# Expert weights of an MoE layer: from split fp32r passes over a short ring to plain fp32 matmuls in column halves and quarters over one ring of 14 slots

## What is computed

```python
def moe_swiglu(h, router, w_in, w_out):
    logits = (hf @ router).astype(jnp.float32)            # 256 tokens, 8 experts
    top_v, top_i = lax.top_k(logits, TOP_K)               # TOP_K = 2
    gates = jnp.sum(jax.nn.one_hot(top_i, N_EXPERTS) * softmax(top_v)[..., None], axis=1)
    for e in range(N_EXPERTS):                            # w_in[e]: 1024 x 7168, w_out[e]: 3584 x 1024
        y = y + gates[:, e:e + 1] * swiglu(hf, w_in[e], w_out[e])
```

## Time and profile before

| | us |
|---|---|
| median of 3 runs (lowest, highest) | 1541.47 (1537.42, 1542.13) |
| the profiled execution | 1540.51 |
| its span, first to last instruction | 1538.8 |
| TensorE busy in it | 1463.6 |
| VectorE busy in it | 1148.2 |
| ScalarE busy in it | 810.3 |

### The profile page before, as it was taken

One profiled execution on the slowest core, in us unless ns is written; L12 is line 12 of the kernel. 1 busy time (PEld: TensorE's weight loads), 2 busy tenths in 40 slices (PEclk: granted clock), 3 DMA queues, 4 the chain that ended last, 5 costly groups with the idle time before them and its releaser, 6 DMA issues.

```text
span 1538.8 us, 20581 instructions
## 1 busy us (share of the span) xinstructions
PE 1463.6 (95%) x6931; PEld 1077.8 (70%) x6931; DVE 1148.2 (75%) x1406; ACT 810.3 (53%) x986; POOL 62.2 (4%) x47
## 2 busy tenths in 40 slices
PE   5999999999999999999999999899998999999997
PEld 5788877888878977756666667575665766666665
DVE  6989998887888878756676677584767756676687
ACT  2544545444446657645464555463645645564565
POOL 0222300000000120000000000000000000000000
PEclk9999999999999999999999999999999999999999
DMA  9987676888976352999999999899999999999993
GB/s 329 346 295 259 248 271 235 300 284 311 320 258 209 106 207 102 335 357 396 400 387 396 398 387 391 317 394 397 398 396 352 361 395 397 397 380 399 396 392 138
DMA packets 220826, 501.51 MB, mean 326 GB/s; under 512 B 9744, under 2 KB 40640, under 8 KB 206400
## 3 DMA queue, kind: packets, MB, share of 16 engines
q1 hardware_dynamic: 219568, 500.29, 88.0%
q10 hardware_dynamic: 1168, 0.07, 0.0%
HBM read 499.28 MB, written 1.05 MB: 325 GB/s over the span
## 4 chain that ended last, share of the span: by engine, by line
PE 55%; DMA 19%; DVE 15%; issue 6%; ACT 4%; DVEq 0%; SPq 0%; ACTq 0%
DMA raw<-in_moe_w_in 13%; PE ps L615 12%; PE ps L617 11%; PE ps L616 11%; PE ps L1155 6%; DVE acc L1916 4%; DMA ada<-in_ada_w 3%; PE ps L1191 3%; DVE w_lo L1897 3%; ACT w_hi L1762 2%; DMA raw<-in_moe_w_out 2%; DVE w_lo L2364 2%; PE ps L915 1%; PE ps L917 1%; PE ps L919 1%
## 5 line engine op out<-in xcount | busy, mean ns | idle before, releaser
L2364 DVE TENSOR_TENSOR w_lo<-raw,w_hi 128x1024 fp32r<-128x1024 f32 x411 | 482.8, 1219 | 156.5 <-ACT w_hi L1762 155.5
L1762 ACT ACTIVATE w_hi<-raw 128x1024 fp32r<-128x1024 f32 x411 | 417.6, 1053 | 195.9 <-DMA raw<-in_moe_w_out 90.1
L615 PE MATMUL ps<-w_hi,RA 128*128 128x512 f32 x1008 | 405.8, 403 | 22.7 <-DVE w_lo L2364 15.7
L617 PE MATMUL ps<-w_hi,RA 128*128 128x512 f32 x1008 | 394.6, 391 | 0.0
L616 PE MATMUL ps<-w_lo,RA 128*128 128x512 f32 x1008 | 394.2, 391 | 0.0
L615 PEld LDWEIGHTS ps<-w_hi,RA 128*128 128x128 f32 x1008 | 190.3, 189 | 88.0 <-DVE w_lo L2364 39.0
L1897 DVE TENSOR_TENSOR w_lo<-raw,w_hi 128x1024 fp32r<-128x1024 f32 x171 | 214.3, 1263 | 13.6 <-ACT w_hi L1435 13.1
L1435 ACT ACTIVATE w_hi<-raw 128x1024 fp32r<-128x1024 f32 x171 | 174.8, 1053 | 88.1 <-PE ps L617 55.4
L617 PEld LDWEIGHTS ps<-w_hi,RA 128*128 128x128 f32 x1008 | 189.9, 188 | 41.2
L616 PEld LDWEIGHTS ps<-w_lo,RA 128*128 128x128 f32 x1008 | 190.3, 189 | 37.2 <-issue 0.7
L1916 DVE SCALAR_TENSOR_TENSOR acc<-ada,cond,acc 128x512 f32<-128x512 f32 x189 | 152.1, 805 | 3.7 <-DMA ada<-in_ada_w 0.7
(11 more groups left out here) (337 smaller groups left out, 1351.7 us busy)
## 6 DMA issues: line engine op xcount, KB each, us to landing
raw<-in_moe_w_in SPq DMA_DIRECT2D x224, 1024.0 KB
raw<-in_moe_w_out SPq DMA_DIRECT2D x112, 1024.0 KB
ada<-in_ada_w SPq DMA_DIRECT2D x46, 1024.0 KB, 7.4
raw<-in_ff_w_in SPq DMA_DIRECT2D x44, 512.0 KB
raw<-in_ret_w_in SPq DMA_DIRECT2D x16, 1024.0 KB
raw<-in_ff_w_out SPq DMA_DIRECT2D x11, 1024.0 KB
raw<-in_ret_w_in SPq DMA_DIRECT2D x16, 512.0 KB
raw<-in_ret_w_out SPq DMA_DIRECT2D x8, 1024.0 KB
```

The lines of the kernel that those rows point to most:

```text
L615: pe.matmul(out, a_hi, b_hi, start=first, stop=False)
L617: return pe.matmul(out, a_lo, b_hi, start=False, stop=last)
L1762: act.activation(w_hi[:, ring(rn), cols], raw[:, (U_MOE + rn) % RAW, cols], ACT.Copy).then_inc(hi_done, 1)
L2364: v.tensor_tensor(w_lo[:, ring(rn), cols], raw[:, (U_MOE + rn) % RAW, cols], w_hi[:, ring(rn), cols].bitcast(f32), ALU.subtract).then_inc( ...
```

## The change

All experts' weights now stay whole: no split, no w_hi and w_lo, no fp32r passes in the expert stage. One ring of 14 slots of 1024 KB takes the six slots of `raw`, the six that the rings w_hi and w_lo make up (as `w_whole`), and the two of `ada`, the buffer of the modulation weights. A slot is given back by TensorE alone (raw_gone). The first use of a slot waits for what used its memory before.

```diff
-CAP = P // 2
-MOE_U = RAW * UNITS
+CAP, CAPF = 64, 96
+MOE_U = 6 * UNITS
+SLOTS = 14
...
             def freed(r, p):
 
-                if r < RAW and p == 0:
+                if not (isinstance(p, int) and p == 0 and r < SLOTS):
+                    sp.wait_ge(raw_gone, gone(r - SLOTS + 1, p))
+                elif r < RAW:
                     sp.wait_ge(lo_done, before_half(U_MOE + r - RAW + 1))
...
+                elif r < RAW + 2 * RING:
+                    sp.wait_ge(w_used, before_half(U_MOE - RING + (r - RAW) // 2 + 1))
                 else:
-                    sp.wait_ge(lo_done, moe_half(old, turn) + 2)
+                    sp.wait_ge(ada_step, 27 * 8)
+                    if r == SLOTS - 2:
+                        sp.wait_ge(ss_ok, NB * 3 + 2)
+                    else:
+                        sp.wait_ge(gbc_done, 4)
+
+            def load_up(n, p, e):
                 u = UNIT[n][2]
                 for k in range(4):
-                    r = max(RAW * n - 2, 0) + k
+                    r = up_slot(n) + k
                     freed(r, p)
-                    sp.dma_start(slot4(U_MOE + r, 0, TW), cols_of(w_ab, e * D + k % 2 * 4 * P, k // 2 * FE + u * TW, TW))\
-                      .then_inc(w_in[(U_MOE + r) % RAW], 32)
+                    slot = moe_raw(r).rearrange("p (t g n) -> p t g n", t=2, g=2)
+                    for g in range(2):
+                        sp.dma_start(slot[:, :, g, :], w_ab[ds(e * D + k * 2 * P, 2 * P), ds(g * FE + u * TW, TW)]
+                                     .rearrange("(t p) n -> p t n", p=P)).then_inc(m_in[r % SLOTS], 16)
```

```diff
+            def up(n, p, i):
...
+                for k in range(4):
+                    if k % 2 == 0:
+                        arrived(r + k // 2, p)
+                    kc = 4 * i + k
+                    for g in range(2):
+                        last = pe.matmul(ps[64 * g:64 * g + 64, Z, :], h[:, kc, 0:CAP], w[k // 2][:, k % 2, g, :], start=kc == 0,
+                                         stop=kc == KC - 1)
+                    if few and k % 2:
                         last.then_inc(raw_gone, 1)
+                if few:
+                    return
+                for k in range(4):
+                    kc = 4 * i + k
+                    for q in range(4):
+                        last = pe.matmul(ps[32 * q:32 * q + 32, ZO, 0:S], h[:, kc, CAP:CAPF],
+                                         w[k // 2][:, k % 2, q // 2, q % 2 * S:(q % 2 + 1) * S], start=kc == 0,
+                                         stop=kc == KC - 1)
+                    if k % 2:
+                        last.then_inc(raw_gone, 1)
```

```diff
+            def transpose_z(n, p):
+
+                few = UNIT[n][0]
+                pe.wait_ge(esa_ok, UNITS * p + n + 1)
+                for c in range(4):
+                    last = pe.transpose(ps[:, ZT, c * P:(c + 1) * P], zs[:, 0, c * P:(c + 1) * P], ident[:, :])
+                if not few:
+                    pe.wait_ge(eg_ok, full_no(n, p))
+                    for t in range(2):
+                        last = pe.transpose(ps[:, ZOT, t * P:(t + 1) * P], zs[:, 1, t * P:(t + 1) * P], ident[:, :])
+                last.then_inc(eT_done, 1)
...
             def step(n, p):
...
+                rows_there(n, p)
+                up(n, p, 0)
                 between(n, p)
...
+                up(n, p, 1)
...
                 pe.wait_ge(eTl_ok, UNITS * p + n)
...
+                first_down(n - 1, p)
+                down(n - 1, p)
                 emptied(n, p)
...
+                transpose_z(n, p)
```

The output of a full expert lies in halves and quarters too, so gating is done piece by piece, and the last expert's halves are gated after all of the last `down`:

```diff
+            def gated_rows(k, bank):
+
+
+                cols = slice(k * TW, (k + 1) * TW)
+                if k == 0:
+                    return v.tensor_tensor(y32[0:CAP, cols], ps[0:CAP, bank, :], gate_f[0:CAP, cols], ALU.mult)
+                for j in range(2):
+                    of = slice(CAP + 32 * j, CAP + 32 * j + 32)
+                    ins = v.tensor_tensor(y32[32 * j:32 * j + 32, cols], ps[of, bank, :], gate_f[of, cols], ALU.mult)
+                return ins
+
+            def gated_overflow(k):
+
+                for q in range(2 * k, 2 * k + 2):
+                    of, cols = slice(32 * q, 32 * q + 32), slice(q * S, (q + 1) * S)
+                    ins = v.tensor_tensor(y32[CAP:CAPF, cols], ps[of, YO, 0:S], gate_f[of, cols], ALU.mult)
+                return ins
```

More of the change, by code:

```diff
@@ L66, with up_slot, down_slot, full_no @@
 SCATTER_FEW = {19: 0, 37: 1, 54: 2}
[L69 to L85, removed]
-def gone(r, p):
[L90 to L99, removed]
+Z, ZO, YW, ZT, Y, YO, ZOT = range(7)
+def up_slot(n):
+    return max(6 * n - 2, 0)
+def down_slot(n):
+    return 6 * n + 8 if n < UNITS - 1 else MOE_U - 2
+def gone(r, p):
+    return r + MOE_U * p
+def full_no(n, p):
+    return sum(f <= n for f in FULL_AT) + NF * ET * p
 def before_step(steps, n):
@@ L167, in trunk @@
         ids = sb("ids", [P, NE], i32)
+        with nc.sbuf_tensor("w_hi", [P, RING, HALF], f32r) as w_hi, nc.sbuf_tensor("w_lo", [P, RING, HALF], f32r) as w_lo:
+            pass
+        w_whole = sb("w_whole", [P, 2, RING, HALF])
         ps = ctx.enter_context(nc.psum_tensor("ps", [P, 8, 512], f32))
@@ L1149, in up_few @@
-            def up_few(r, p, bank):
-                for h in range(2):
-                    q = (U_MOE + r + h) % RAW
-                    pe.wait_ge(w_in[q], raw_full(r + h, p))
-                    for t in range(4):
-                        kc, half = 4 * h + t, slice(t % 2 * CAP, (t % 2 + 1) * CAP)
-                        last = pe.matmul(ps[half, bank, :], f_h32[:, kc, :], raw[:, q, t * TW:(t + 1) * TW], start=kc < 2,
-                                         stop=kc >= KC - 2)
-                    last.then_inc(raw_gone, 1)
@@ L1159, in down @@
-            def down(r, p, first, last_one):
-                for kc in range(4):
-                    s, t = ring(r + kc // 2), kc % 2
-                    arrived(r + kc // 2, p, t)
-                    for n in range(2):
-                        cols = slice(t * D + n * TW, t * D + (n + 1) * TW)
-                        last = passes(ps[:, 4 + n, :], eT_hi[:, kc, :], eT_lo[:, kc, :], w_hi[:, s, cols],
-                                      w_lo[:, s, cols], first and kc == 0, last_one and kc == 3)
-                    last.then_inc(w_used, 1)
@@ L1170, in down_direct @@
-            def down_direct(r, p, first):
-                for kc in range(4):
-                    s, t = (U_MOE + r + kc // 2) % RAW, kc % 2
-                    if t == 0:
-                        pe.wait_ge(w_in[s], raw_full(r + kc // 2, p))
-                    for n in range(2):
-                        cols = slice(t * D + n * TW, t * D + (n + 1) * TW)
-                        last = pe.matmul(ps[:, 4 + n, :], e32[:, kc, :], raw[:, s, cols], start=first and kc == 0,
-                                         stop=False)
-                    if t == 1:
-                        last.then_inc(raw_gone, 1)
@@ L1183, in down_few @@
-            def down_few(r, p, first, last_one):
-                for h in range(2):
-                    q = (U_MOE + r + h) % RAW
-                    pe.wait_ge(w_in[q], raw_full(r + h, p))
-                    for k in range(2):
-                        for t in range(2):
-                            half = slice(t * CAP, (t + 1) * CAP)
-                            last = pe.matmul(ps[half, 6 + k, :], fe32[:, 2 * h + t, :],
-                                             raw[:, q, t * D + k * TW:t * D + (k + 1) * TW],
-                                             start=first and h == 0, stop=last_one and h == 1)
-                    last.then_inc(raw_gone, 1)
```

576 lines of the change are left out of this document (207 added, 369 removed).

## The result

The changed kernel takes **1518.2 us** (median of four runs, 1515.4 to 1523.3) against 1541.1 of the kernel before (four runs beside it, 1537.4 to 1542.1): a ratio of 0.987, 95% interval 0.984 to 0.989. It is faster by 23 us, 1.3%; 61 were forecast, and 1518 lies outside the range of 1464 to 1506. The profiled execution's span is 1513.6 us, 25.2 less than before's 1538.8.

What follows compares the result with a forecast made beforehand. Expert-weight transfers were taken as the bound; an earlier stream (19 us), closed holes (33) and a shorter tail (10) cut the span from 1538.8 to 1477.0, so 1480 us was forecast, range 1464 to 1506.

Steps and rivals of the forecast that it cites:

- what bounds the kernel before: Expert stage of the old kernel: weight transfers at their ceiling of 397 GB/s are the bound, despite TensorE busy 95%.
- the stream: Expert weights: flow resumes at 607.5 after transfer 14's slot returns at 605.5; 322 transfers take 850.5 us, last weight at 1458.0.
- 24 matmuls in column halves, 0.2215 us each, 5.3 us: TensorE's half-array matmuls in a full unit, priced from 32 in 7.09 us; part of 12.3 us a unit.
- The quarters: The 48 quarter-array matmuls of a full unit: 0.053 to 0.390 us each, taken as 0.08, so 3.8 us.
- TensorE waits for weights a third of the time: Expert stage: units of 12.3 and 6.4 us sum to 565 us of TensorE work against 850.5 of transfers.
- the changes of tiling: TensorE switching between whole array, halves and quarters: some seven times a full unit, 2.5 us in all.
- that dearer case: Each tiling change costing a whole matmul's 0.6 us: a full unit is 13.7 us, still below its transfers' 15.8.
- TensorE becomes the bound: Expert stage: TensorE cold throughout, 1028 us of units, total 1658 us, slower than before; chance 0.03.
- point of decision: Expert stage: the change turns out slower than before from 16.4 us of TensorE a unit on average; forecast sum 10.1.
- The other cause, the clock: TensorE at a lower clock while waiting for slots: half the units cold gives 1484, cold throughout 1658 at chance 0.03.
- A gather, a fold or a scatter, below 10 us a piece, doesn't reach the queue: Expert stage: eleven or so transfers stay queued, 29 us, so the holes in the transfer rate close, worth 33 us.
- The tail: Work after the last weight: last matmul 2.7 us behind it, then 16 us, together 19 where 29 were needed.

Runs made afterwards that it cites:

- experiment 7: The kernel before, with each up transfer loading half its bytes, splits and matmuls all kept: 1501.5 us.
- experiment 1: The changed kernel with only 12 of the 48 quarter matmuls of a full unit issued, loads and order the same: 1491.9 us.
- experiment 2: The changed kernel with each up slot loading half its rows and the matmuls reading that half twice: 1518.3 us.
- experiment 3: The changed kernel with the 16 up half matmuls issued twice in each of 21 few-units: 1646.5 us.
- experiment 4: The changed kernel with each scatter moved from between its unit's two up parts to behind the second: 1502.3 us, ratio 0.977 to the kernel before.
- experiment 8: The changed kernel with the scatter behind both up parts and half-size up loads together: 1500.0 us.
- experiment 5: The changed kernel with a ring of 8 slots, and of 6, in place of 14: 1521.9 us and 1544.7 us.

## Why the prediction was wrong

**Right: what bounds the kernel before, and in the main the stream.** The transfers were its bound (experiment 7: 38 us go with half of the up bytes). From 660 to 1460 the rate is 395, where the kernel before has 387; the 383 of the earlier trace rows are of a longer stretch, with both ends of the stage in it. The queue's issues in the kernel after, which answer to the earlier trace rows:

```profile
589.99 6.32 SPq L505 DMA_DIRECT2D ada<-in_moe_w_in  x4
604.37 1.24 SPq L513 DMA_DIRECT2D raw<-in_moe_w_out  x2
```

Transfer 14 goes out at 604.4. This execution was 3.7 us ahead in the shared part in front of it (SyncE's last issue for the attention's output weights stands at 532.5 for 536.2), so that is 608.1 on the clock of the profile before, where 605.5 was worked out: the slot waits for all eight half matmuls of the first up part, now 3.6 us. From there the slots come back at TensorE's pace: from 610 to 660 us the rate is 338 GB/s, not 397, and with few quarters (experiment 1) it is 378. The end of the stream, 1471.6 + 3.7 = 1475.3, is 17 us later than the forecast's 1458.0.

**Wrong: "24 matmuls in column halves, 0.2215 us each, 5.3 us".** This is the step that failed. The earlier trace rows show "32" for L1155 of one few-unit; the code issues 16 in it. I took a row's count for the time of one, and the code's count for the product. The term is 10.8 us a full unit for 5.3, and 10.7 a few-unit for 5.3. The quarters were bounded per record too: 0.058 a record is near the lower bound of 0.053, so the reasoning from halves that overlap in full to quarters that will too held, but as 0.116 a matmul they are 5.6 us for 3.8. By 17.2 and 11.2 us a unit "TensorE waits for weights a third of the time" turns over: experiment 2 takes a third of the bytes away without effect, experiment 1 takes some of TensorE's work away and gives 26 us, and experiment 3 adds some and pays for it by the price of two records.

The comparison with the kernel before was at hand and wasn't made: the earlier trace rows give a full unit 72 passes of one record each at 0.23, 16.9 us with its transposes. The new unit is 17.2. The change made TensorE no lighter; it took 525 us of busy time off VectorE and 417 off ScalarE (page), and neither was the bound.

**Too dear: the changes of tiling.** I put 0.35 us on each, 2.5 a full unit. The 7.09 us of 32 half records, and the 3.65 of 16 in the unit shown, run to the end of the last record, so 16 more records cost 3.44 us: 0.215 each, and not 7.09 / 32 = 0.2215. The same difference between 32 and 24 quarter records (1.93 and 1.50 us) gives 0.054 each. So 48 half records are 10.3 us, 96 quarter records 5.2 and six transposes 0.7, 16.2 in all; the unit takes 17.2, and its seven changes take the 1.0 between them, about 0.15 each. This hid 1.5 us of the error a unit. The Trainium skill, "TensorEngine Tiling (Array Packing)", Key Properties, says that a change of tiling mode drains TensorE. The trace fits a drain, at 0.15 us, but not one of a whole record's duration (0.6 us). The prediction's sum for that dearer case has a slip: 9.8 + 7 x 0.6 is 14.0 us a full unit, not 13.7; nothing else hangs on it.

**The rival that came true in part** is "TensorE becomes the bound", at 0.03, for a cause that I had not given it: the price of a matmul, not a cold clock. Its point of decision was well placed: slower than before from 16.4 us a unit. The stage has 16.0, and (16.4 - 16.0) x 56 = 22 us are about the gain. That the true price leaves the stage at 16.0, below 16.4 and not above it, nobody had worked out, so that the kernel still came out faster, as forecast, is in part luck. The other cause, the clock, is a minor one: 0.98 in the stage, from the waits at the scatters; with them gone 1.00 (experiment 4). Waits for weights didn't turn TensorE cold either: in experiment 1 there are 74 of them of at most 1.1 us each, and the clock from 660 to 1460 is 0.98 as in the changed kernel.

**"A gather, a fold or a scatter, below 10 us a piece, doesn't reach the queue"** is true in the main and misled me. The queue ran on at 397 GB/s past the scatter at 790 us; once it was reached, from 980 to 1000, at 346, where the kernel with the late scatter has 400. But with TensorE as the bound each wait at a scatter counts in full, whatever the queue does: 16 us in experiment 4.

**The tail** has 42 us behind the last weight for 19. Its second part was right: 16 us were forecast from the last matmul to the end, and 1497.6 to 1513.6 are 16. The first part, 2.7, is 26, since it is no tail but TensorE's arrears. In experiment 1, where the transfers are the bound, the tail is 26 in all (1464 to 1489.9), so even there the forecast of 19 is 7 short. Its rows show where: the second slot of unit 54's down projection was to land 5.3 us before the end of the stream, and TensorE waits for it until 1464.27, the end itself. From there the matmuls of both down projections, the transposes and 1.2 us for the product run one behind another to 1473.8. Why these last transfers land so close together wasn't followed further.

**The account of the 25.2 us of span:** the time from the first up projection to the last matmul went from 923.7 us (603.75 to 1527.4) to 897.9, the first up projection began 4.1 earlier, and the end chain is 4.7 longer (16.1 for 11.4): 25.8 + 4.1 - 4.7 = 25.2. Against the forecast of 1477.0 the kernel after ends 36.6 later, and all of that is the last matmul: forecast for 1460.7, it ends at 1497.6.

What is left open: the changed design needs 878 us of TensorE in the stage (experiment 8) and the kernel before takes 883 with half of its up bytes (experiment 7, 605.0 to 1488.4). Their units, 17.2 and 11.2 us for 16.9 and 11.6, fit this, but no run took TensorE's work out of the kernel before, so it isn't known how far its transfers alone would have let it come. Nor is it shown how the first 23 us divide. The new units on a ring of six win nothing (experiment 5), so the room is needed; no run has the old units with more room.

## What to carry to other kernels

Before a duration from a trace is multiplied by a number of instructions from the code, count one loop in both: if the rows hold twice as many records as the code has matmuls, the price is per record. "Which resource is the bound after the change" is decided by time per unit on each side, and when the two come close (16.0 and 15.2 us here), every wait on the engine that is the bound counts in full; look for those first, and test both sides by taking away part of each. Matmuls that share the array are cheap only beside each other: leave out three of four, and the one left costs what the four did (experiment 1). When the work behind an expert's last product becomes more and shorter instructions, give the engine that waits for it more work to cover it: here one loop part later was worth 16 us.

## What the runs showed of the hardware

- An fp32 matmul stands as two MATMUL records, in halves and quarters of the array and in the whole array alike (the broadcast L680: four records for two matmuls); a transpose stands as one. Between starts a record in column halves (128x64 by 512) takes 0.215 us, so the matmul 0.43; in column quarters (128x32 by 256) 0.054, the matmul 0.11. Two halves side by side take the 0.86 us of one whole-array matmul 512 wide. Four quarters side by side take 0.43, half of that for half the width; a quarter alone takes about as long as the four (four records in 0.98 us with the changes around them, experiment 1).
- A change between halves, quarters and whole array costs about 0.15 us (seven in a unit of 17.2).
- VectorE's time for a piece goes by its columns, not by its partitions: 64x512 took 0.67 us, 32x512 0.70 (two in 1.39), 32x256 0.43 (two in 0.85). Rows folded into 32 partitions at a time are dear on it.
- One core read weights at a mean of 397 GB/s for 800 us on end (experiment 4, 660 to 1460), with up slots in two transfers of 512 KB and down slots in one of 1024 KB; the kernel before, with 1024 KB throughout, has the same 396 to 400 in its undisturbed slices.
- After 3.9 us without work TensorE's sixteen half records took 4.93 us for 3.65. The kernel of experiment 4, which hardly has these waits, had a granted clock of 1.00 for the whole stage.
